# A long expert placed last, gate halves made ahead of the last item's product, y rows gathered from inside the experts stage

## What is computed

```python
h2 = rmsnorm(x, g_ffn)
# router: one of 4 groups, then the 2 best of its 8 experts; 2 * 1056 = 2112 (token, expert) pairs
for each expert e of 32, over the tokens sent to it:
    y = (silu(h2 @ w_gate[e]) * (h2 @ w_up[e])) @ w_down[e]      # 1024 -> 512 -> 1024
x = x + gate1 * y1 + gate2 * y2                                  # the two rows of each token
gate = sigmoid(rmsnorm(x, g_ple) @ w_ple_gate + b_ple_gate)      # 1024 x 1024
x = x + gate * (p @ w_ple_proj)
y = rmsnorm(x, g_final)
```

## Time and profile before

| | us |
|---|---|
| median of three runs | 1168.76 (1167.81 to 1170.07) |
| the profiled execution | 1167.64 |
| its span in the trace | 1165.9 |
| PE busy | 1075.2 (92%) |
| PE weight loads | 616.0 (53%) |
| DVE / ACT / POOL busy | 510.8 / 510.0 / 281.1 |
| moved by DMA | 300.32 MB, mean 258 GB/s |

### The profile page before, as it was taken

The page is one execution under the profiler, slowest core; times in us unless marked ns, Lnnn a source line. Parts: engine busy times, 40 slices in busy tenths (PEclk is TensorE's granted clock), DMA queues, the critical chain, the costliest instruction groups (busy, mean ns, idle before and its releaser), DMA issues. The chain is left out here.

```text
span 1165.9 us, 17839 instructions
## 1 busy us (share of the span) xinstructions
PE 1075.2 (92%) x5269; PEld 616.0 (53%) x5270; DVE 510.8 (44%) x660; ACT 510.0 (44%) x690; POOL 281.1 (24%) x303
## 2 busy tenths in 40 slices
PE   2799996889999886999999999999999999969996
PEld 2799995778888642333333333333333333328885
DVE  4457999996222171213213212311312312356886
ACT  4343554766222144335435535534633535423432
POOL 1045886687000011111011101111101111023320
PEclk9899999899999878999999999999999999989999
DMA  7041753212113748999999999999999999965541
GB/s 226 1 136 55 200 140 139 66 63 96 60 73 132 283 177 320 397 380 337 395 397 358 399 397 384 374 396 396 361 395 397 361 397 397 402 248 172 208 145 41
DMA packets 149297, 300.32 MB, mean 258 GB/s; under 512 B 12032, under 2 KB 42784, under 8 KB 149259
## 3 DMA queue, kind: packets, MB, share of 16 engines
q1 hardware_dynamic: 134907, 264.69, 61.8%
q0 software_dynamic: 6512, 22.29, 5.5%
q10 hardware_dynamic: 7840, 12.85, 2.9%
HBM read 261.72 MB, written 38.06 MB: 257 GB/s over the span
## 5 line engine op out<-in xcount | busy, mean ns | idle before, releaser
L1951 PE MATMUL ps_gate_up<-weights,x_turned 128*64 128x512 f32 x1568 | 349.6, 598 | 1.4 <-issue 0.7
L106 ACT COPY weights<-raw_weights 128x2048 f32 (+1 forms) x99 | 186.1, 1899 | 102.8 <-issue 46.8
L1951 PEld LDWEIGHTS ps_gate_up<-weights,x_turned 128*64 128x64 f32 x1568 | 109.5, 137 | 206.9 <-issue 205.8
L106 DVE COPY weights<-raw_weights 128x2048 f32 x93 | 114.6, 1233 | 217.8 <-PE ps_gate_up L1951 85.8
L1964 PE MATMUL ps_y<-weights,h_turned 128*64 128x512 f32 x784 | 179.0, 598 | 0.9 <-ACT h_turned L1871 0.9
L431 POOL TENSOR_TENSOR conv_pool_taps<-conv_pool_taps,tap_product 128x448 f32<-128x448 f32 (+1 forms) x88 | 134.7, 1531 | 41.3 <-ACT tap_product L518 31.7
L1911 DVE TENSOR_TENSOR hidden<-ps_gate_up,act_gate 128x256 f32<-128x256 f32 x49 | 20.8, 425 | 222.9 <-ACT act_gate L1862 214.8
L115 POOL COPY token_ids<-item_tokens 128x1 int32 (+1 forms) x48 | 8.8, 183 | 446.9 <-PE ps_x L1938 446.9
L850 DVE SCALAR_TENSOR_TENSOR taps_bank<-a_ext,par,taps_bank 128x640 f32<-128x640 f32 (+1 forms) x128 | 101.6, 794 | 3.3
L1964 PEld LDWEIGHTS ps_y<-weights,h_turned 128*64 128x64 f32 x784 | 52.2, 136 | 93.3 <-issue 92.2
L518 ACT ACTIVATE tap_product<-a_ext,par 128x448 f32<-128x448 f32 (+1 forms) x104 | 75.9, 740 | 50.4 <-POOL conv_pool_taps L431 38.9
(11 more groups left out here) (285 smaller groups left out, 1546.0 us busy)
## 6 DMA issues: line engine op xcount, KB each, us to landing
raw_weights<-w_exp_gate SPq DMA_DIRECT2D x128, 512.0 KB
raw_weights<-w_exp_up SPq DMA_DIRECT2D x128, 512.0 KB
raw_weights<-w_exp_down SPq DMA_DIRECT2D x64, 1024.0 KB
y_rows<-y_tile ACTq DMA_DIRECT2D x98, 128.0 KB, 5.4
y_rows<-zero_rows SPq DMA_DIRECT2D x16, 512.0 KB, 6.2
x_rows<-x_tile SPq DMA_DIRECT2D x9, 512.0 KB, 2.7
h_rows<-h_tile SPq DMA_DIRECT2D x9, 512.0 KB, 2.9
mixer<-x_rows SPq DMA_DIRECT2D x9, 512.0 KB, 4.5
```

Of the source, the lines that this page charges most:

```text
L106: copy(S.work[s][:, :], raw).then_inc(S.w_ready[s], 1)
L1951: last = pe.matmul(ps_gu[side[j], :, :], x_t[:, c, side[of]], w[:, :, share(D_EXP, j)], start=(k == 0), stop=(k == KD - 1))
```

## The change

Three things change.

```diff
+def gather_y(pool, S, t):
+
+    for k, (dst, got) in enumerate(((S.room[0:2], S.y1_in), (S.room[2:4], S.y2_in))):
+        pool.indirect_dma_start(out=dst[t % 2], out_offset=None, in_=S.y_rows[:, :],
+                                in_offset=bass.IndirectOffsetOnAxis(ap=S.out_row[:, k, t:t + 1], axis=0)).then_inc(got[t % 2], 16)
...
-                iota(spread[:, 2:].rearrange("p (a b) -> p a b", b=6), [[1, 5], [5, 6]], 2, 0)
+                by_six = spread[:, 2:].rearrange("p (a b) -> p a b", b=6)
+                iota(by_six[:, :, 0:3], [[1, 5], [5, 3]], 2, 0)
+                iota(by_six[:, :, 3:6], [[-1, 5], [5, 3]], 21, 0)
...
-                for rows, src in zip((S.g_ple_rows, S.b_ple_rows, S.g_final_rows), gains):
-                    sp.dma_start(rows[:, :], src.partition_broadcast(P)).then_inc(S.ple_rows_loaded, 16)
-                sp.wait_ge(S.ple_rows_loaded, 48)
+                for rows, src, loaded in zip((S.g_ple_rows, S.b_ple_rows, S.g_final_rows), gains,
+                                             (S.g_ple_loaded, S.ple_rows_loaded, S.ple_rows_loaded)):
+                    sp.dma_start(rows[:, :], src.partition_broadcast(P)).then_inc(loaded, 16)
...
                 with pool.Fori(1, n_last) as i:
                     gather(i + 1)
+                pool.wait_ge(S.ple_split, 4)
+                pool.wait_ge(y_stored, n_last * 16 * SIDES + 32 * SIDES)
+                pool.sem_inc(S.waits_met, 1)
+                for t in range(2):
+                    gather_y(pool, S, t)
...
                 with act.Fori(1, end) as i:
                     iteration(i)
-                iteration(end, final=True)
                 gate_hi(2)
                 gate_hi(3)
+                iteration(end, final=True)
                 leave_y(end)
                 store_y(end)
...
                 with dve.Fori(1, end) as i:
                     iteration(i)
-                iteration(end, final=True)
-                for j in range(SLOTS):
-                    dve.wait_ge(S.proj_stored[j], 16 * len(range(j, LATE, SLOTS)))
                 for n, s in enumerate((0, 1)):
                     dve.wait_ge(S.raw_loaded[s], LANDED[s] * EXPERTS + 16)
                     dve.wait_ge(w_ready[s], EXPERTS)
                     dve.tensor_copy(S.ple_hi[s][:, :], S.raw[:, 0, s, :]).then_inc(S.ple_split, 1)
                     dve.wait_ge(S.ple_split, 2 * n + 1)
-                    dve.wait_ge(w_ready[DOWN[s]], EXPERTS)
+                    gate_lo(dve, S, s)
+                iteration(end, final=True)
+                for n, s in enumerate((2, 3)):
+                    dve.wait_ge(S.ple_hi_ready, n + 1)
+                    dve.wait_ge(w_ready[DOWN[n]], EXPERTS)
                     gate_lo(dve, S, s)
...
-                fetch(0)
-                fetch(1)
                 power(0, 0)
...
+                    if t == 0 and j == 0:
+                        dve.wait_ge(S.g_ple_loaded, 16)
...
+                    if t == 0:
+                        dve.wait_ge(S.ple_rows_loaded, 32)
...
-                gate_lo(dve, S, 2)
-                gate_lo(dve, S, 3)
-                dve.wait_ge(S.ple_split, 6)
                 combine(0, 0)
```

More of the change, by code:

```diff
@@ L2018, in embedding_gate @@
         ps_h1 = ps_h[1][:, :, :].rearrange("p k n -> p (k n)")
-        y1_in, y2_in, out_stored = ([sem(f"{n}{j}") for j in range(2)] for n in ("y1_gathered", "y2_gathered", "out_stored"))
+        y1_in, y2_in, out_stored = S.y1_in, S.y2_in, [sem(f"out_stored{j}") for j in range(2)]
         proj_loaded = S.proj_loaded
@@ L2069, in fetch @@
                 def fetch(t):
[L2071 to L2074, removed]
+                    pool.wait_ge(y1_in[t % 2], loads_of(t - 2))
+                    pool.wait_ge(y2_in[t % 2], loads_of(t - 2))
+                    pool.wait_ge(x3_ready, done_in(t - 2))
                     pool.sem_inc(S.waits_met, 1)
[L2076 to L2079, removed]
+                    gather_y(pool, S, t)
                 def power(j, t):
@@ L2351, in build @@
             S.ple_hi = [sb(f"ple_hi{s}", [P, PIECE], F32R) for s in range(4)]
-            S.ple_lo = [sb(f"ple_lo{s}", [P, PIECE], F32R) for s in range(2)]
+            S.ple_lo = [sb(f"ple_lo{s}", [P, PIECE], F32R) for s in (2, 3)]
             S.work = [sb(f"weights{s}", [P, PIECE]) for s in PIECES]
@@ L2366, in build @@
         S.late_rows = [w[:, h * D:(h + 1) * D] for w in S.work[3:5] for h in range(2)]
-        S.ple_lo += [sb(f"ple_lo{s}", [P, PIECE], F32R) for s in range(2, 4)]
+        S.ple_lo = [sb(f"ple_lo{s}", [P, PIECE], F32R) for s in (0, 1)] + S.ple_lo
         S.g_ple_rows, S.b_ple_rows, S.g_final_rows = (sb(n, [P, D]) for n in ("g_ple_rows", "b_ple_rows", "g_final_rows"))
-        S.ple_rows_loaded = whole.enter_context(nc.semaphore("ple_rows_loaded"))
+        S.ple_rows_loaded, S.g_ple_loaded = (whole.enter_context(nc.semaphore(n)) for n in ("ple_rows_loaded", "g_ple_loaded"))
+        S.y1_in, S.y2_in = ([whole.enter_context(nc.semaphore(f"{n}{j}")) for j in range(2)] for n in ("y1_gathered", "y2_gathered"))
         experts(nc, S, blocks(i["w_ple_gate"]), blocks(i["w_ple_proj"]), (i["g_ple"][0], i["b_ple_gate"][0], i["g_final"]))
```

## The result

| | before | after |
|---|---|---|
| median of the runs | 1169.41 (4 runs) | 1195.61 (4 runs, 1194.45 to 1200.08) |
| the profiled execution | 1167.64 | 1196.36 |
| its span | 1165.9 | 1194.6 |
| PE busy | 1075.2 | 1085.0 |
| first item's tokens transposed to end of the last product | 574.5 | 598.6 |

The changed kernel is slower: ratio 1.0225, 95% interval 1.0203 to 1.0246. The forecast was 1187.4 with a range of 1178 to 1195. The direction came as forecast, and so did the loads that starve PE in the stage; the border behind the stage grew where the forecast had it shrink. The time is 8.2 above the forecast and 0.6 above its range.

What follows compares the result with a forecast made beforehand. PE and the DMA loads were both taken as near their limits in the experts stage. Run losses 19.5, plus clock 2.3, minus border 3.1, on 1167.64 gave 1186.3, median 1187.4; 8-in-10 range 1178 to 1195.

Steps and rivals of the forecast that it cites:

- The loads' lead and the run of six: Experts stage, six singles in a row: late weights stop PE behind the fourth, fifth and sixth, 15.1 us lost.
- The run of four: Near the stage's end, four singles before a three-item expert: 5.2 us lost, net 4.4 since the old 0.79 goes.
- the forecast's own sum: Run of four: lateness 2.4 behind the third single, plus 5.6, minus 2.83 of slack, gives 5.2 us lost.
- The clock: Slow matmul restarts behind the stalls: only a run's last stall costs; 0 to 4.6 us, 2.3 taken.
- the rule, named there: Trainium skill on HAM oscillation: matmul bursts split by waits for DMAs each begin at the lower clock.
- the bound of 4.6: Upper limit of the clock term, for slow restarts behind the last stalls of two runs; 2.3 was taken.
- The splits ahead of the last item: End of the experts stage: ACT's two and DVE's four splits, moved ahead of the last item, cost nothing.
- The border: Experts stage to gate: barrier about as before, PE's two waits go, products start at 1046.6, 3.1 us gained.
- Barrier at 1026.6 + 6.0 + 0.4: Stage's end: last y rows stored at 1026.6, four gather issues 6.0, then 0.4; barrier at 1033.0.
- its 1186.3: Forecast for the profiled execution: 1167.64 + 19.5 + 2.3 - 3.1; the median was put 1.1 higher.
- the prediction's own bounds: Lowest and highest sums of the forecast's terms, 1182 to 1198, for the whole kernel.
- The clock paid in full: Second rival, experts stage: each of four new stalls pays its slow start, 9.2 instead of 2.3, time 1194.3; chance 0.14.

Runs made afterwards that it cites:

- the table alone: Kernel before with only its table of places changed to the new order of experts; 1190.29, ratio 1.0178.
- the run in the middle: Kernel before with the fourth group alone reversed, six singles in a row in the middle, last places as before; 1189.2, ratio 1.0157.
- The old table: Changed kernel with the table of places of before, keeping the early splits and early gathers; 1184.79, ratio 1.0118.
- the 22.6 with the gathers behind the barrier: Border of the changed kernel with its four gathers put back behind the barrier; 1187.94, ratio 1.016.
- y rows first: Kernel before; ACT copies and stores the last y rows ahead of piece 3's split, SP no longer waits for the gains; 1170.39, ratio 1.0000.
- the spread order: Kernel before with a three-item expert last and the singles spread, no run over four in the other places; 1176.1, ratio 1.0051.

## Why the prediction was right or wrong, step by step

**The loads' lead and the run of six: right.** Forecast 3.9 + 5.6 + 5.6 = 15.1, measured 3.92 + 5.66 + 5.66 = 15.24, with DMA share 1.04 and 395 to 397 GB/s. That the order does it, and nothing else of the change, is shown by the table alone (+24.3 in the stage) and by the run in the middle (the same three stalls).

**The run of four: right in kind, a little too dear.** Forecast 5.2, measured 3.82. By the forecast's own sum that is a lateness of 3.82 - 5.6 + 2.83 = 1.05 behind the third single, that of a usual group, where 2.4 was taken. The prediction named a two-item expert ahead of the three-item one as what helps; that this is the cause is not shown. One figure of the working is wrong, and nothing of the sum rests on it: an expert of two items moves 6.29 + 2 * 0.52 = 7.33 MB, 18.5 us at 397 GB/s, so it wins 4.6 and not 5.3.

**The clock: a term mis-sized.** Forecast 2.3 for one restart in all; measured 2.58 behind the run of six and 3.53 behind the run of four, 6.1. That restarts between stalls are absorbed was right: their distance is 17.22, the loads' pace, though each of their products takes 8.7 to 8.8. So was the rule, named there, that every stall ends in a slow start: all four did. What was wrong was to halve the bound of 4.6, and the bound itself: an idle of 2.92 ahead of the last transposition was already enough for a slow restart, and the start of the product is late too, 1.40 behind the transposition instead of 0.37. Why PE waits there the profile doesn't say ("issue"), and it stays open.

The stage: 15.24 + 3.82 - 0.79 + 6.11 = 24.4, measured 24.1, forecast 21.8. The miss of 2.3 is about the restarts' 3.8 less the run of four's 1.4.

**The splits ahead of the last item: right.** They cost nothing here: the stage took 598.6 with them and 598.73 with the table alone. The old table shows what covers them: the two further items of a long last expert.

**The border: the step that failed.** It is the "0.4" in "Barrier at 1026.6 + 6.0 + 0.4". Its other pieces held or came out cheaper: POOL's first gather began 4.64 behind the product (forecast 4.2), the issues took 4.7 (forecast 6.0, under even the bound of 5.6), the products came 13.8 behind the barrier (forecast 13.55), with the two waits gone. But the barrier came 7.0 behind the last issue. I had taken it that a block ends when its engines have issued all; it ended 2.4 behind the landing of the last gather, though it did not wait for SP's direct DMA. Forecast 24.2 for the border, measured 30.1: 5.9 too little. With the stage's 2.3 and the 1.8 of the later start that is 10.0, by which the profiled execution missed its 1186.3. The median missed by 8.2; that this equals 5.9 + 2.3 to the tenth is luck, since the profiled execution lies above the median here and lay under it before. The bounds of the border, 22.9 to 28.5, had no room for it, since both ends went by issues. The stated range ended at 1195, under the 1198 that the prediction's own bounds added up to. No row of before could show it, since nothing of POOL's was under way at that barrier; that is why the term needed a bound of its own, from the landing of a gather. Where the border's gain comes from was wrong too. It was to come from the gathers; but the table alone, with the gathers behind the barrier, has the border 3.6 shorter, and with the early splits 4.7. Even without the 7.0 the early gathers would have had nothing to win: 30.1 - 7.0 = 23.1, against the 22.6 with the gathers behind the barrier.

Of the rivals none came alone. The clock paid in full (1194.3) came near the time for the wrong reason: it wanted four slow restarts of 2.3 on the path, and the trace has two on the path, together 6.1.

## What to carry to other kernels

When loads and computation are both near their limits, the order of long and short items is a budget of lead: write down what each item wins or loses against the loads (here +4.6 for two items, by the traffic of 18.5 us, and -5.6 for one) and keep every run of short ones within it, because the last stall of a run also brings a slow restart. Before gathers are moved ahead of a barrier, ask whether their transfers, not only their issues, will be through by then, and which work of other engines stood beside them until now. A wait that a barrier hides is shortened by moving off whatever lands last (here two rows of gains), not by adding transfers in front of it.

## What the runs showed of the hardware that was not expected

- The end of a block waited for the landing of indirect DMAs that POOL had issued and nothing in the block waited for: 7.0 behind the last issue, and 11.2 with busier queues, though POOL itself was free. In five traces it lay 2.4 to 2.5 behind the last landing. A direct DMA of SP did not hold the barrier: it landed 1.0 behind it (y rows first, one trace).
- An issue of a gather of 512 KB took 0.94 with DVE idle, and 2.37 and 1.89 beside DVE's subtractions of two inputs, each ending 0.81 to 0.83 behind a subtraction.
- After an idle of 2.8 to 4 us, at granted clocks of 0.91 and 0.83 over the stretches of 20 us, 32 matmuls took 8.5 to 8.8 and 9.5 to 9.6 instead of 7.09, and began 1.0 later behind the transposition. In the spread order an idle of 1.06 was enough for 8.78; at the start of the stage an idle of 2.01, behind the first product, was followed by 7.09 in the kernel before and the changed one. So the length of the last idle alone doesn't decide it; what does stays open.
- The last y rows' two stores of 128 KB landed in 2.3 on idle queues; before they took 5.6.
